# Order of two VectorE steps in the first layer's attention

## What is computed

```python
def probs(c):
    logits = jnp.einsum('bqhd,bkhd->bhqk', q[:, qs:qe, :, c], keys[:, :ke, :, c]).astype(jnp.float32)
    return masked_softmax(logits * scale + bias, mask)

diff_map = probs(0) - lam * probs(1)
return jnp.einsum('bhqk,bkhe->bqhe', diff_map.astype(vals.dtype), vals[:, :ke])
```

## Time and profile before

| quantity | value |
|---|---|
| device time, three runs | 970.66, 975.79, 976.01 us (median 975.79) |
| profiled execution: span | 969.9 us; the page gives no device time of its own for it |
| PE busy | 918.8 us, 95% of the span |
| DVE, ACT, POOL busy | 402.4, 307.2, 155.7 us |
| chain that ended last | PE 85%, DVE 6%, DMA 4%, ACT 3% |
| the 24 attention items of layer 1 | about 119 to 190 us after the span's start |
| the first experts' matmuls | from 247 us |

### The profile page before, as it was taken

The page is one execution under the profiler, slowest core; times in us unless marked ns, Lnnn a source line. Parts: engine busy times, 40 slices in busy tenths (PEclk is TensorE's granted clock), DMA queues, the critical chain, the costliest instruction groups (busy, mean ns, idle before and its releaser), DMA issues.

```text
span 969.9 us, 11879 instructions
## 1 busy us (share of the span) xinstructions
PE 918.8 (95%) x4620; PEld 563.3 (58%) x4620; DVE 402.4 (41%) x848; ACT 307.2 (32%) x627; POOL 155.7 (16%) x220
## 2 busy tenths in 40 slices
PE   4999989999999999998899999999999999999997
PEld 3877756778434444443477777777786444443443
DVE  4757366435212323223738643454535122222223
ACT  4553467623211111112434445464332110111110
POOL 3424323210000000000312254433010000000000
PEclk9999999999999999999899999999899999999999
DMA  9833632169699999999434364353867999999994
GB/s 310 268 131 133 203 133 73 52 230 411 266 424 419 422 421 420 419 407 421 157 98 130 118 198 125 100 167 108 334 275 288 408 422 421 421 420 420 421 421 185
DMA packets 56778, 271.55 MB, mean 280 GB/s; under 512 B 5840, under 2 KB 6080, under 8 KB 32144
## 3 DMA queue, kind: packets, MB, share of 16 engines
q1 hardware_dynamic: 47824, 242.65, 63.5%
q0 software_dynamic: 8896, 28.09, 9.1%
HBM read 260.95 MB, written 9.77 MB: 279 GB/s over the span
## 4 chain that ended last, share of the span: by engine, by line
PE 85%; DVE 6%; DMA 4%; ACT 3%; issue 1%; POOL 1%; SPq 0%; DVEq 0%
PE ps L1537 22%; PE ps L1555 12%; PE ps L1099 7%; PE ps L1101 7%; PE ps L1100 7%; PE ps L1569 2%; PE ps L1154 2%; PE ps L1155 2%; PE ps L1570 2%; PE ps L1318 2%; PE ps L1322 2%; PE ps L1511 2%; DMA w_raw<-in_moe_w_up 1%; DMA w_raw<-in_diff_w_in 1%; PE ps L1126 1%
## 5 line engine op out<-in xcount | busy, mean ns | idle before, releaser
L1537 PE MATMUL ps<-w_extra,xT 128*64 128x512 f32 x512 | 162.6, 594 | 2.5 <-DMA w_raw<-in_moe_w_up 2.5
L1537 PE MATMUL ps<-w_raw,xT 128*64 128x512 f32 x320 | 142.0, 593 | 0.0
L1099 PE MATMUL ps<-w_hi,hT_hi 128*128 128x512 f32 x224 | 94.7, 423 | 5.7 <-DVE hT_lo L1682 5.4
L1660 DVE TENSOR_TENSOR w_lo<-w_raw,w_hi 128x2048 fp32r<-128x2048 f32 x33 | 75.1, 2287 | 42.5 <-ACT w_hi L763 42.5
L1101 PE MATMUL ps<-w_hi,hT_lo 128*128 128x512 f32 x224 | 89.9, 401 | 0.0
L1100 PE MATMUL ps<-w_lo,hT_hi 128*128 128x512 f32 x224 | 89.7, 400 | 0.0
L1537 PE MATMUL ps<-w_more,xT 128*64 128x512 f32 x192 | 85.1, 594 | 0.0
L1537 PEld LDWEIGHTS ps<-w_raw,xT 128*64 128x64 f32 x320 | 43.2, 137 | 71.2 <-issue 71.2
L1555 PE MATMUL ps<-w_extra,hidT 128*64 128x512 f32 x240 | 82.8, 596 | 0.0
L1537 PEld LDWEIGHTS ps<-w_extra,xT 128*64 128x64 f32 x512 | 50.2, 137 | 52.2 <-issue 52.0
L763 ACT ACTIVATE w_hi<-w_raw 128x2048 fp32r<-128x2048 f32 x33 | 62.4, 1909 | 43.8 <-PE ps L1155 37.9
(11 more groups left out here) (297 smaller groups left out, 1630.8 us busy)
## 6 DMA issues: line engine op xcount, KB each, us to landing
w_extra<-in_moe_w_up SPq DMA_DIRECT2D x35, 1024.0 KB, 16.6
w_extra<-in_moe_w_down SPq DMA_DIRECT2D x30, 1024.0 KB, 17.6
w_extra<-in_moe_w_gate SPq DMA_DIRECT2D x29, 1024.0 KB, 17.1
w_raw<-in_moe_w_gate SPq DMA_DIRECT2D x25, 1024.0 KB, 16.2
w_raw<-in_moe_w_down SPq DMA_DIRECT2D x21, 1024.0 KB, 16.0
w_raw<-in_fox_w_in SPq DMA_DIRECT2D x16, 1024.0 KB, 5.4
w_raw<-in_moe_w_up SPq DMA_DIRECT2D x15, 1024.0 KB, 12.8
w_more<-in_moe_w_up SPq DMA_DIRECT2D x14, 1024.0 KB, 20.2
```

The lines of the kernel that those rows point to most:

```text
L1099: mm(out, a_hi, b_hi, start=start, stop=False)
L1537: ins = mm(ps[j * CAP:(j + 1) * CAP, bank, :], xT[:, kb, j * CAP:(j + 1) * CAP], buffer(U.slot)[:, k * F:(k + 1) * F], start=(kb == 0), st ...
L1660: v.tensor_tensor(w_lo[:, U.slot, :], w_raw[:, U.slot, :], w_hi[:, U.hslot, :].bitcast(F32), ALU.subtract).then_inc(lo_ready, 1)
```

## The change

In the first layer (`l == 0`), DVE's iteration j now runs `mix(j)` ahead of `take_o(j-2)`. Before, `take_o(j-2)` came first. Nothing else in the order changes, and the second layer keeps its order.

```diff
                 for j, p, t in its:
+                    if l == 0 and j >= 1:
+                        mix(j, p, t)
                     if j >= 2:
                         take_o(*its[j - 2])
-                    if l == 1 or j >= 1:
+                    if l == 1:
                         mix(j, p, t)
                     if j + 2 < len(its):
                         row_max(*its[j + 2])
```

## The result

The changed kernel takes 967.2 us (median of 11 runs, 963.99 to 973.33) beside 974.09 for the kernel before (11 runs, 970.66 to 976.01): ratio 0.9949, 95% interval 0.9929 to 0.997. It is 0.5% faster. A second timing on another occasion gave 0.9947 (0.9924 to 0.9971). The forecast was 970.6 against 975.8, a gain of 5.2 us; the ratio stands for 5.0. The two medians differ by more, 6.9 us. The measured 967.2 is 3.4 us under the forecast time: 1.7 of that is the median before, 974.1 over 11 runs where the forecast started from 975.8 over three, and 1.7 is this larger difference of the medians.

The account below looks back on a forecast made before the run. The prediction took a ring of waits between PE and DVE in the attention as the bound. Five steady triplets at 0.8 us (4.0) plus 1.2 for items 2 to 5 gave 5.2: 975.8 to 970.6 us, range 965.0 to 975.0.

Parts of the forecast that it names:

- The ring of two engines: Attention: PE's `values` releases DVE's `take_o`, then `mix`, which releases PE's `probs_T`; 0.29 us of waiting hidden at t = 2.
- Printed idle: Low bound of the gain: PE's printed waits alone, 3.5 us over five triplets and 0.4 at item 2, 3.9.
- The walk of one triplet: PE's queue laid out step by step with new waits for `dT` and `diag`: triplet 7.80 to 7.0 us, 0.8 saved.
- upper bound: Every wait goes and none comes: 1.22 us a triplet, 6.1, and 1.2 for the start, 7.3 in all.
- The order of what is late: Late next in a triplet: ACT's `dT` behind the cached keys' copy, then DVE's `row_max` ahead of `mix`.
- Number of triplets: Items 6 to 20, five triplets, 4.0 us; items 2 to 5, 1.2; items 21 to 23 nothing; sum 5.2.
- Reaching the end: The expert weight stream moves forward with the attention, so the whole 5.2 us saving reaches the end.
- take_o's new place hidden: Behind `mix`, `take_o`'s 0.35 us is covered by PE's `scores` and `probs_T`, at least 0.49 + 0.27 us.
- Rival 1: Little arrives since ACT's busy queue eats the lead: 973 to 975.8 us; chance 0.12.
- Rival 3: Slower: late exponentials make `mix` hold back `take_o` and `row_max` on DVE, at most 7.7 us, 983.5; chance 0.03.
- Rival 4: No gain, because the stream of expert weights decides: 975.8 us; chance 0.07.
- Rival 2: Clock falls at 122.0 to 131.5 and 192 to 222 us stay away: 2.8 us more, 967.8; chance 0.14.

Follow-up runs that it names:

- e7_pool: Against the changed kernel, POOL issues the load of cached values after the statistics of the heads, not before: 7.02 us a triplet, 968.95 us.
- e8_both: Against the changed kernel, the edits of e5_copy and e6_mix2 together: 6.69 us a triplet, 962.3 us, ratio 0.9885 to the kernel before.
- e5_copy: Against the changed kernel, ACT's copy of `dT` of t = 0 goes ahead of the cached keys' copy: 7.04 us a triplet, 967.55 us.
- the last kernel: The kernel of e8_both and e10_both, the changed kernel with two further edits: 6.69 us a triplet, ratios 0.9885 and 0.9887 to the kernel before.
- e1_t0: Against the kernel before, the changed order for items with t = 0 alone: 7.45 us a triplet, 970.87 us.
- e4_last: Against the changed kernel, `take_o(j-2)` goes behind `row_max(j+2)` too, with an added wait ahead of `mix`: 9.10 us a triplet, 983.25 us.
- e6_mix2: Against the changed kernel, `mix` of t = 2 runs one iteration earlier, ahead of `row_max` for t = 0: 7.02 us a triplet, 969.13 us.
- e10_both: The kernel of e8_both timed again beside the changed kernel: 965.44 us, ratio 0.9887 to the kernel before.

## Why the prediction held

- **The ring of two engines** was right: what went away is PE's wait ahead of `probs_T` and DVE's ahead of `take_o`. Isolated, the order of the t = 0 items is worth 0.34 us a triplet, where the prediction read 0.29 of hidden waiting from 1.32 against 1.03. The other 0.05 stands one step on: L1322 started 0.26 after a waiting L1287 and starts 0.21 after one that doesn't wait.
- **Printed idle** was rightly only the low bound. All waits of the old triplet together are worth 7.79 - 6.69 = 1.10 us, 5.5 in five triplets, of which 3.5 was printed. That the measured gain of these five, 3.52, is the printed 3.5 is an accident: new waits took back the other 2.0, 0.33 a triplet for `dT` and 0.07 for the slowed `diag`.
- **The walk of one triplet** gave 7.0; it is 7.09, and 7.02 where `diag` takes its 0.25 us (e7_pool, and the last two of the changed kernel's five). Its wait for ACT's `dT` came. It costs 7.02 - 6.69 = 0.33 us: L1318 starts 0.50 behind L1287 where 0.27 is the unwaited distance, and the next scores start 0.42 behind L1318 where 0.32 is. Most of that is not printed, so the sign that I named, a printed idle of 0.4, is not in the timeline. Its second wait, for `diag`, is none where `diag` is not slowed.
- **What the prediction had wrong** is how soon PE goes on unwaited. It gave the two `scores` 0.32 and 0.53 us, and with no wait at all they need 0.42 and 0.63 (e8_both). In the walk this hardly shows, because it took the starts behind them from ACT and DVE. In the upper bound it does: 1.22 a triplet was never there, 1.10 is the most.
- **The order of what is late** was right: without the `dT` wait alone (e5_copy) a triplet gains 0.05, since `diag` is next, and without both (e8_both) 0.40.
- **What the walk missed** is 0.07 a triplet, 0.35 us in all: `diag` slowed by POOL.
- **Number of triplets.** The five steady ones gave 3.5 for 4.0. For items 2 to 5 I took 1.2, and the order did give 15.03 - 13.80 = 1.2 (the changed kernel took 13.80 in both its profiles). Together 4.7 for 5.2. The term that was over-sized is the triplet's saving, 0.70 for 0.8, and most of the difference is the slowed `diag`. That the timed gain came out at 5.0 is nearer than the mechanism alone accounts for.
- **Reaching the end** was right: first load and end of the attention moved alike, and the wait for the expert stream did not grow.
- **take_o's new place hidden** was right: no PE wait for it in the changed trace, and one step later it costs 9.10 - 7.09 = 2.0 us a triplet.
- **Rival 1** (ACT eats the lead) didn't happen: ACT is busy 5.87 of 7.05 and costs the 0.33 above. **Rival 3** (slower) needed exponentials that come late; DVE's idle ahead of L1775 in the attention is none. **Rival 4** fell with the first point on reaching the end. **Rival 2**, the clock, did add to the profiled execution: the first fall was missing (1.00 for 0.89), about 1.2 us. That the change took it away is not shown, and two things speak against it: e7_pool, with the changed order on DVE, has the fall (0.80), and the mean clock over all runs is 0.9877 for 0.9869. The rule of the Trainium skill that the prediction cites ("TensorE: Matmul & The Clock Gate", section on the psum-queue depth-cycling), that frequent small idles between groups of matmuls make the clock swing, found no support in the steady triplets: those with three waits each and those with none ran at 1.00.
- **The expected verdict**, same within 1%, held; the interval, 0.9929 to 0.997, still lies wholly below 1.

What stays open is why the last kernel's mean clock is higher (0.9901, 12 runs, against 0.9869 over 29). The fall in the first triplets is in the profiles of the kernel before and of e7_pool, in small in those of e1_t0 (0.98) and e8_both (0.99), and in neither profile of the change, and a few executions can't settle what decides it. Also not separated is the 1.0 us after the attention in the first profile; a second profile of the changed kernel has 792.6 instead of 790.4 us there, more than the 791.4 of the kernel before, so it is likely spread.

## What to carry to other kernels

If an in-order engine takes a finished result and then prepares the next input of the engine that made it, prepare first and take second, as long as the maker has other work to cover the taking; and test each kind of item by itself, because a step whose input is held up elsewhere gains nothing alone (t = 1: 0.00). Read the worth of such a move from start-to-start distances with and without a wait, on the waiting instruction and on the one behind it, not from printed idle. Compare steady stretches of traces, which repeat to 0.01 us, when the total is spread over 10 us by the clock.

## What the hardware showed unasked

- The DVE instruction that writes `diag` (fp32, SBUF to SBUF, 128 x 64) takes 0.25 us, and 0.31 to 0.53 where POOL is in the middle of issuing the load of cached values (148.99 to 149.74 against 149.25 above). In the kernel before, the two never met in the steady triplets. With POOL's issue moved it was 0.25 always, so POOL's issue is the cause. The lengths follow a pattern. In all 22 lengthened cases, over seven profiles, the instruction started during the issue and ended within 0.03 us of the issue's end. Three times in e4_last it started so late in the issue (0.56 to 0.65 of 0.75 us) that it ended after it anyway, and it took 0.25. And 12 times in e6_mix2, e8_both and e10_both it started 0.04 to 0.17 us before POOL's issue of a load of cached keys, and took 0.25 or 0.26. So it is held only by an issue that started first, and until this one ends.
- `L1848`, which reads PSUM, took its usual 0.34 in the issue shown above. The Trainium skill ("SBUF — State Buffer", section "SBUF: two separate sides") says that DVE and GpSimd share one pair of ports under an exclusive lock, and tells of DVE holding up the descriptors that GpSimd writes; here the same lock would work the other way round. The first-come order above fits a lock; that it is this one is argued, not shown.
- The granted clock of a single core differs between runs of one program, 0.981 to 0.993 for the kernel before (29 runs) and 0.981 to 0.992 for the changed one (23 runs), and accounts for most of their spread: per 0.001 of clock the span moves by 0.8 to 1.0 us.
